# One expert stage of a two-block model kernel: 64 of 512 tokens by gathered rows, 448 by dense products with sums kept in PSUM

## The reference, cut to what matters

```python
s1 = einsum('thc,hkc->thk', q[:, :, 0], sub_keys1); s2 = einsum('thc,hkc->thk', q[:, :, 1], sub_keys2)
v1, i1 = top_k(s1, 16); v2, i2 = top_k(s2, 16)
vc, ic = top_k((v1[..., :, None] + v2[..., None, :]).reshape(T, 8, 256), 16)
idx = e1 * 128 + e2                     # per token: 8 heads x 16 picks
gate = softmax(vc)
pre = einsum('td,tkd->tk', x, expert_u[idx])
out = einsum('tk,tkd->td', gelu(pre) * gate, expert_v[idx])
```

## Time and profile before

| What | Value |
|---|---|
| Median of 3 runs | 3835.03 us (3834.25 to 3838.55) |
| Profiled execution, first to last instruction | 3830.8 us (its own whole time is not listed apart from this span) |
| TensorE busy | 3606.3 us, 94% of the span |
| VectorE busy | 2645.0 us, 69% |
| ScalarE, GpSimd busy | 1414.4 us and 1412.7 us, 37% each |
| Mean granted TensorE clock | 0.976 of full speed |

### The profile page before, as it was taken

The page is one execution under the profiler, slowest core; times in us unless marked ns, Lnnn a source line. Parts: engine busy times, 40 slices in busy tenths (PEclk is TensorE's granted clock), DMA queues, the critical chain, the costliest instruction groups (busy, mean ns, idle before and its releaser), DMA issues. The chain is left out here.

```text
span 3830.8 us, 55657 instructions
## 1 busy us (share of the span) xinstructions
PE 3606.3 (94%) x18886; PEld 2929.9 (76%) x18886; DVE 2645.0 (69%) x5198; ACT 1414.4 (37%) x2042; POOL 1412.7 (37%) x608
## 2 busy tenths in 40 slices
PE   8878999999999899999998989889998989989999
PEld 5746787788888788888887766678887877668877
DVE  7654899988888699999997756674455026755440
ACT  2443233345545323233323247632223133753331
POOL 3023344333333344444442326432222322444443
PEclk9989999999999999999999999999999999999999
DMA  5403444345545755555544480232111114032322
GB/s 212 142 12 132 156 147 140 126 136 186 194 151 194 253 194 195 189 192 195 193 164 158 137 165 12 70 107 66 60 60 49 60 61 134 7 121 88 95 79 89
DMA packets 248451, 490.54 MB, mean 128 GB/s; under 512 B 49124, under 2 KB 125924, under 8 KB 243341
## 3 DMA queue, kind: packets, MB, share of 16 engines
q1 hardware_dynamic: 227660, 447.95, 35.7%
q10 hardware_dynamic: 20672, 41.07, 2.9%
HBM read 411.59 MB, written 73.68 MB: 127 GB/s over the span
## 5 line engine op out<-in xcount | busy, mean ns | idle before, releaser
L433 POOL TENSOR_TENSOR ahead_low<-w_raw,ahead_high 128x1024 fp32r<-128x1024 f32 (+1 forms) x159 | 420.8, 2647 | 888.0 <-ACT ahead_high L369 888.0
L229 PE MATMUL psum<-h_high,ahead_high 128*128 128x512 f32 (+1 forms) x1504 | 540.3, 359 | 1.5 <-POOL ahead_low L433 1.5
L230 PE MATMUL psum<-h_low,ahead_high 128*128 128x512 f32 (+1 forms) x1504 | 538.1, 358 | 0.0
L231 PE MATMUL psum<-h_high,ahead_low 128*128 128x512 f32 (+1 forms) x1504 | 535.8, 356 | 0.0
L1945 POOL TENSOR_TENSOR pick_u_low<-pick_u_raw,pick_u_high 128x1024 fp32r<-128x1024 f32 x128 | 309.6, 2419 | 558.5 <-ACT pick_u_high L2022 558.5
L1809 POOL TENSOR_TENSOR v_low<-v_raw,v_high 128x1024 fp32r<-128x1024 f32 x128 | 334.1, 2633 | 369.5 <-ACT v_high L1806 369.5
L369 ACT ACTIVATE ahead_high<-w_raw 128x1024 fp32r<-128x1024 f32 (+1 forms) x159 | 178.0, 1119 | 740.8 <-PE psum L231 704.7
L229 PE MATMUL psum<-h_high,pick_u_high 128*128 128x512 f32 x1024 | 414.8, 405 | 1.4 <-POOL pick_u_low L1945 1.4
L229 PE MATMUL psum<-a_high,v_high 128*128 128x512 f32 x1024 | 399.1, 390 | 10.2 <-DVE a_low L2267 10.2
L230 PE MATMUL psum<-h_low,pick_u_high 128*128 128x512 f32 x1024 | 404.2, 395 | 0.0
L231 PE MATMUL psum<-h_high,pick_u_low 128*128 128x512 f32 x1024 | 401.4, 392 | 0.0
(11 more groups left out here) (395 smaller groups left out, 7236.3 us busy)
## 6 DMA issues: line engine op xcount, KB each, us to landing
pick_u_raw<-in_expert_uT SPq DMA_DIRECT2D x128, 512.0 KB, 3.5
v_raw<-in_expert_v SPq DMA_DIRECT2D x128, 512.0 KB, 4.8
mod_w<-in_w_mod SPq DMA_DIRECT2D x88, 512.0 KB, 3.7
w_raw<-in_ffn_up SPq DMA_DIRECT2D x84, 512.0 KB, 3.5
gelu_dram<-pick_gelu ACTq DMA_DIRECT2D x128, 256.0 KB, 2.0
gates_dram<-gate_plane SPq DMA_DIRECT2D x32, 1024.0 KB, 7.5
p<-gelu_dram SPq DMA_DIRECT2D x128, 256.0 KB, 5.0
g<-gates_dram SPq DMA_DIRECT2D x64, 512.0 KB, 4.3
```

Of the source, the lines that this page charges most:

```text
L229: nc.tensor.matmul(bank, w_high, x_high, start=first, stop=False)
L230: nc.tensor.matmul(bank, w_high, x_low, start=False, stop=False)
L231: return nc.tensor.matmul(bank, w_low, x_high, start=False, stop=last)
L433: nc.gpsimd.tensor_tensor(w_low[r % 2][:, :, :], raw[r % n_raw][:, :, :], w_high[r % 2][:, :, :].bitcast(F32), ALU.subtract).then_inc(k.w_ ...
```

## The change

The last 64 tokens no longer go through the dense products. Token columns 448 to 511 are laid out as 128 partitions (64 tokens, twice: partition 64 and up hold the second half of a token's picks), so each has 64 picks per partition. For each pick one indirect DMA, issued by GpSimd, gathers 128 rows of 1024 floats, first of `expert_u`, later of `expert_v`. VectorE takes the dot product with the token's own row (64 times), ScalarE applies gelu, VectorE multiplies with the gate, and in the second stage VectorE adds each gathered value row times its weight (64 times). A ring of four buffers holds the rows. A float32 matmul with two stacked identities folds both halves and transposes, once per 128 columns of the model width.

The dense products run over 448 columns. There are 7 gate planes of 64 tokens in place of 8, so the parts of `stage_pick` are 64 chunks for finding, 56 for gates, 8 at the end. The tile that holds the gathered tokens is found first. A tile's transposes move from its last chunk to the third chunk of the following tile, its picks are copied half-way through the scan of the next. VectorE's one-hot tiles read their row of numbers from PSUM, and the first of the pair is made for four tokens in one instruction. The copies of the queries for scoring (L2079 and a DMA) go, and the token rows are transposed by 32 float32 matmuls (`turn_h`).

In `stage_values` the sums of all 128 chunks stay in PSUM, and VectorE adds each bank once at the end. The subtraction of the value weights moves from GpSimd to VectorE for all but two chunks. All loops of both stages are written out.

```diff
-        self.gelu = k.nc.dram_tensor("gelu_dram", (N_KEYS, N_KEYS, SEQ), F32).ap()
-        self.gates = k.nc.dram_tensor("gates_dram", (SEQ // GATE_TOK, N_KEYS, N_KEYS, GATE_TOK), F32).ap()
+        self.h_high = k.place("peer_h_high", H_HIGH, KD, SEQ, dtype=FR)
+        self.h_low = k.place("peer_h_low", H_LOW, KD, SEQ, dtype=FR)
+        self.row_ring = [k.place(f"peer_row{r}", at, D) for r, at in enumerate((H_HIGH + KD * SEQ, H_HIGH + KD * SEQ + D, H_LOW + KD * SEQ, H_LOW + KD * SEQ + D))]
+
+        self.gelu = k.nc.dram_tensor("gelu_dram", (N_KEYS, N_KEYS, DENSE), F32).ap()
+        self.gates = k.nc.dram_tensor("gates_dram", (PLANES, N_KEYS, N_KEYS, GATE_TOK), F32).ap()
...
-EIGHT = range(8)
-FIND_CHUNKS, GATE_CHUNKS, LAST_CHUNKS = 14, 16, 8
+ROW_TOK = 64
+DENSE = SEQ - ROW_TOK
+PLANES = DENSE // GATE_TOK
+FIND_TILES = (3, 0, 1, 2)
+FIND_CHUNKS, PLANE_CHUNKS, LAST_CHUNKS = 16, 8, 8
+GATES_AT = len(FIND_TILES) * FIND_CHUNKS
+LAST_AT = GATES_AT + PLANES * PLANE_CHUNKS
...
+ROW_PICKS = PICKS * ROW_TOK // P
+ROW_RING = 4
+DOTS_AFTER = (0, 3, 3, 2)
+DOTS_FOUND = sum(DOTS_AFTER)
...
+    def gather(self, pool, j):
+        if j == 0:
+            pool.wait_ge(self.own_in, 32)
+        if j >= ROW_RING:
+            pool.wait_ge(self.used, j - ROW_RING + 1)
+        rows, n = (self.u, j) if j < ROW_PICKS else (self.v, j - ROW_PICKS)
+        self.nc.gpsimd.indirect_dma_start(self.ring[j % ROW_RING][:, :], None, rows,
+                                          bass.IndirectOffsetOnAxis(ap=self.own[:, 0, n:n + 1].bitcast(U32), axis=0)).then_inc(self.row_in[j % ROW_RING], 16)
+
+    def wait_row(self, dve, j):
+        dve.wait_ge(self.row_in[j % ROW_RING], 16 * (j // ROW_RING + 1))
+
+    def dot(self, dve, n, h, product):
+        self.wait_row(dve, n)
+        self.nc.vector.scalar_tensor_tensor(product, self.ring[n % ROW_RING][:, :], 1.0, h, ALU.mult, ALU.mult, accum_out=self.pre[:, n:n + 1]).then_inc(self.used, 1)
+        dve.wait_ge(self.used, n + 1)
+
+    def add(self, dve, n, acc):
+        j = ROW_PICKS + n
+        self.wait_row(dve, j)
+        row = self.ring[j % ROW_RING][:, :]
+        if n == 0:
+            ins = self.nc.vector.tensor_scalar(acc, row, self.a[:, 0:1], None, ALU.mult)
+        else:
+            dve.wait_ge(self.used, j)
+            ins = self.nc.vector.scalar_tensor_tensor(acc, row, self.a[:, n:n + 1], acc, ALU.mult, ALU.add)
+        ins.then_inc(self.used, 1)
...
+            for c in range(N_KEYS):
+                if c == FIND_CHUNKS + 4:
+                    rows.spread(sp)
+                if c == 2 * FIND_CHUNKS:
+                    sp.dma_start(cond, t["cond"].rearrange("p (c y) -> p c y", y=CTX)).then_inc(cond_in, 16)
+                n, r = divmod(c - LEAD - GATES_AT, PLANE_CHUNKS)
+                if n >= 1 and r < STORE_PARTS:
+                    store_part(n - 1, r)
+                load_u(c)
+                if c == LAST_AT + LEAD:
+                    load_mod(0)
+                    load_mod(1)
+                if c > LAST_AT + LEAD:
+                    load_mod(c - LAST_AT - LEAD + 1)
+            last_mod = N_KEYS - LAST_AT - LEAD + 1
...
+            gathered = 0
+            for c in range(N_KEYS):
+                split(c)
+
+                i, r = divmod(c, FIND_CHUNKS)
+                many = 0
+                if c < GATES_AT:
+                    if r == 5 and i == 1:
+                        many = ROW_RING
+                    if r == 5 and i > 1:
+                        many = DOTS_AFTER[i - 1]
+                elif c == GATES_AT + 2:
+                    many = DOTS_AFTER[-1]
+                elif GATES_AT + LEAD <= c < GATES_AT + LEAD + n_gate:
+                    many = 1
+                for _ in range(many):
+                    rows.gather(pool, gathered)
+                    gathered += 1
...
+            def chunk(c):
+                pe.wait_ge(u_split, c + 1)
+                if c >= 2:
+                    pe.wait_ge(gelu_done, c - 1)
+                for d in range(KD):
+                    mm = split_product(nc, k.psum[:, 5 + c % 2, 0:DENSE], u_high[c % 2][:, d, :], u_low[c % 2][:, d, :],
+                                       f.h_high[:, d, 0:DENSE], f.h_low[:, d, 0:DENSE], d == 0, d == KD - 1)
                 mm.then_inc(pre_done, 1)
...
+            def turn_h():
+                for d in range(KD):
+                    to = k.psum[:, 4 + 3 * (d // 4), d % 4 * P:(d % 4 + 1) * P]
+                    for half in HALVES:
+                        for part, h in enumerate((f.h_high, f.h_low)):
+                            mm = nc.tensor.matmul(to[half, :], h[:, d, DENSE:SEQ].bitcast(F32), k.const("ident"), start=(part == 0), stop=(part == 1))
+                mm.then_inc(rows_turned, 1)
+
             pe.wait_ge(keys_in, 16)
-            pe.sem_inc(pre_done, 2)
-            pe.wait_ge(staged, 16)
-            score()
-            with pe.Fori(0, TILES - 1) as it:
+            score(0)
+            for i in range(len(FIND_TILES)):
                 for r in range(FIND_CHUNKS):
-                    if r == SCORE_CHUNK:
-
-                        pe.wait_ge(best_found, it + 1)
-                        pe.wait_ge(staged, it * 16 + 32)
-                        score()
-                    chunk(it * FIND_CHUNKS, r)
-                turn(it)
-            for r in range(FIND_CHUNKS):
-                chunk((TILES - 1) * FIND_CHUNKS, r)
-            turn(TILES - 1)
-            with pe.Fori(0, TILES) as it:
-                for r in range(GATE_CHUNKS):
-                    chunk(it * GATE_CHUNKS + gates_at, r)
-                    for q in range(per_chunk):
-                        spread(it, r * per_chunk + q)
+                    if r == SCORE_CHUNK and i + 1 < len(FIND_TILES):
+
+                        score(i + 1)
+                    chunk(i * FIND_CHUNKS + r)
+                    if i and r == TURN_CHUNK:
+                        turn(i - 1)
+                    if i == 0 and r == TURN_CHUNK:
+                        turn_h()
+            for q in range(n_gate):
+                chunk(GATES_AT + q)
+                if q == TURN_CHUNK:
+                    turn(len(FIND_TILES) - 1)
+                for g in range(per_chunk):
+                    spread(q * per_chunk + g)
...
+                if i == 0:
+                    nc.vector.scalar_tensor_tensor(rows.all[:, 0, :].bitcast(U32), out[0][:, :], float(N_KEYS), out[1][:, :], ALU.mult, ALU.add).then_inc(rows.found, 1)
+                    dve.wait_ge(picked, 1)
+                    nc.vector.tensor_copy(rows.all[:, 1, :], out[2][:, :]).then_inc(rows.found, 1)
+                    dve.wait_ge(h_rows_ready, 2)
+                for _ in range(DOTS_AFTER[i]):
+                    rows.dot(dve, dots, h_rows[:, :], products[:, :])
+                    dots += 1
...
+            dve.wait_ge(h_rows_ready, 3)
+            for q in range(n_gate):
+                for g in range(q * per_chunk, (q + 1) * per_chunk):
                     b = g % 2
-                    dve.wait_ge(summed, it * per_tile + (g + 1))
+                    if g >= 2:
+                        dve.wait_ge(summed, g - 1)
+                    n = slice(g * group, (g + 1) * group)
+                    nc.vector.tensor_tensor(hot1[b][:, :, :], iota.unsqueeze(1).to_broadcast([P, group, N_KEYS]),
+                                            f.picks[:, 0, n].unsqueeze(2).to_broadcast([P, group, N_KEYS]), ALU.is_equal)
                     for j in range(group):
                         n = g * group + j
-                        nc.vector.tensor_scalar(hot1[b][:, j, :], iota, own[:, 0, n:n + 1], None, ALU.is_equal)
-                        ins = nc.vector.tensor_scalar(hot2[b][:, j, :], iota, own[:, 1, n:n + 1], own[:, 2, n:n + 1], ALU.is_equal, ALU.mult)
+                        ins = nc.vector.tensor_scalar(hot2[b][:, j, :], iota, f.picks[:, 1, n:n + 1], f.picks[:, 2, n:n + 1], ALU.is_equal, ALU.mult)
                     ins.then_inc(hot_ready, 1)
-                dve.wait_ge(hot_ready, it * per_tile + per_tile)
-
-            V.restart(dve)
+                rows.dot(dve, dots, h_rows[:, :], products[:, :])
+                dots += 1
+                if q == 2 * TURN_CHUNK:
+                    store_picks(len(FIND_TILES) - 1)
...
+            def step(c):
+                if c >= 2:
+                    act.wait_ge(b.v_in[c % 4], 16 * (c // 4 + 1) + b.chunks_before)
+                    if c >= 4:
+                        act.wait_ge(done.sem, done.at(c - 3))
+                    b.round_v(act, c)
+                act.wait_ge(gated, c + 1)
+                if c >= 4:
+                    act.wait_ge(done.sem, done.at(c - 3))
+                nc.scalar.activation(a_high[c % 4][:, :], a_full[c % 4][:, :], ACT.Copy).then_inc(a_high_ready.sem, 1)
+
+            for c in range(N_KEYS):
+                step(c)
...
+            for n in range(ROW_RING, ROW_PICKS):
+                rows.gather(pool, ROW_PICKS + n)
...
+            def chunk(c):
```

(44 more changed lines are left out.)

474 lines of the change are left out of this document (207 added, 267 removed).

## The result

The changed kernel takes 3704.01 us (median of 4 runs, 3702.11 to 3708.9) where the kernel before took 3836.79 beside it: ratio 0.966, 95% interval 0.9648 to 0.9672. Its profiled span is 3700.3 us against 3830.8, so 130.5 us less. The forecast was 156 less.

A forecast was written before the change was run, and what follows sets the result against it. TensorE was taken to set the time, VectorE close behind in two of four windows. Values -78.1, last chunks -0.3, finding and gates -76.4, start -1.2 sum to -156 us: 3835 to 3679 us, own range 3660 to 3705.

The forecast's parts named there:

- Columns pay: Finding and gates: narrower matmuls shorten both windows from 811.4 to 735 us, 76.4 less, with TensorE waiting 26 us for VectorE.
- Values, -78.1: Value stage: 128 chunks each 0.63 us shorter, 80.6 us less, minus folds and a less covered tail; 78.1 us less.
- the line between 344 and 512 columns: Dense products: interpolating matmul pace between these widths gives 200.4 ns at 448 columns for values, 203.3 for the first stage.
- The tail behind TensorE: End of the value stage: a tail of squares that gets less cover, 0.6 us more.
- The folds: End of the value stage: 8 float32 folds, two records each at about 120 ns, 1.9 us more.
- Last eight chunks, -0.3: Last chunks before the values: 5.4 us less, but TensorE then waits 5.1 us longer; 0.3 us less.
- modulation chain: Between last chunks and values: modulation loads and VectorE's columns, a chain of 50.7 us that does not shrink.
- Start and rest: Start: 1.2 us less, as the copy of queries goes; what lies around the span was left as it is.
- Slower gathers: Rival, GpSimd: gathers hold its queue, deciding from 6.6 us each; at 7.3 us each the kernel takes 3886 us; chance 0.06.
- VectorE bounds the gates: Rival, gates: one-hots or dot still held by GpSimd's subtraction, step 7.7 us, 58 us more, 3737 us; chance 0.15.
- Columns don't pay: Rival, dense products: matmuls of 448 columns keep the pace of 512, kernel 3815 us; chance 0.02.
- VectorE not late: Rival, finding: fewer collisions or hidden dots shrink the 26 + 2 us to 4, kernel 3655 us; chance 0.08.

## Why the prediction was right, and where it was off

The forecast of 3679 (own range 3660 to 3705) stood beside 3704: the case was right, the size 25 us off, at the edge of its range. It forecast a gain of 156 us, and 130.5 were measured between the profiled spans. By its own steps:

- **Columns pay.** Gates and finding: forecast 735 us for the two windows, measured 735.1 (452.9 to 1188.0). First spread 364 us after VectorE's first scan, measured 362.6; wait 26, measured 25.6; step 6.65, measured 6.70. The gathers cost GpSimd 0.96 us each (1.5 taken), hidden. The eight dots took 14.8 us (16 taken), six of them 1.3 and two 3.5, and the rest of VectorE's work within 1 us of its 348; how the single terms of that rest came out was not measured.
- **Values, -78.1.** The term that was mis-sized. TensorE is the bound and VectorE at 59% (some 65% forecast), but the pace is 202.7 ns in place of 200.4: 3072 x 2.3 = 7 us. (The prediction gave VectorE 5.9 us of work a chunk before, which adds up durations that overlap; the earlier trace rows have 686.51/128 = 5.36.) The step that failed is the line between 344 and 512 columns. At 448 it is one of two paces, and neither lies on that line. The tail behind TensorE was given 0.6 us and took 4.4 more (17.5 against 13.1): with one chunk per visit the banks finish 0.82 us apart, GpSimd's four additions of squares (1.43 us from one to the next) fall behind, and TensorE waits 2.2 us for them. Its eight sums then take 5.2 us in place of 3.6, the first of them at a granted clock of 0.5. With two chunks per visit the tail was 13.6. The folds took no more than their 1.9 us: 625.8 less 3072 x 0.2027 leaves 3.1 us, with 1.5 for the half clock of the first chunk in it.
- **Last eight chunks, -0.3.** This step failed. I forecast 42.6 us of chunks and a gap of 15, with the modulation chain setting the end. Measured 53.4 and 14.8. The gap's number was right by luck, for a wrong reason: it hangs on GpSimd, whose two value subtractions the change had moved behind the last chunk and whose block end comes 5.65 us late after gathers. The 10.8 us in the chunks are, in the main, the context sums and one load. The sums took 3.6 us before and now 5.4 behind a wait of 2.95, 4.8 more. The wait for a u part that the DMA engines bring late is 3.9, and the chunk at half clock behind it 1.6 more. Moving the sums took out their whole 8.1 us, also the 3.6 that were in the forecast. The chain's 50.7 us I took as fixed, and it was (50.2 here, from the first load at 1191.63); that what holds it, 18 MB in 54 us, would hold the u loads too once a chunk took 4.9 us in place of 5.5, I had not asked.
- **Start and rest.** The start was to gain 1.2 us and lost 1.1; the rest of the kernel took 3.0 us more. Neither need be the change's: between kernels with the same instructions there, the first score came at 443.1 to 449.0 and the rest took 1797.6 to 1803.0.
- Sum of the misses: 2.3 at the start, -0.5 in finding and gates, 10.5 around the last chunks, 10.3 in values and tail, 3.0 in the rest: 25.6 of 25.5.
- **Rivals.** Slower gathers: refuted, 0.96 us against a threshold of 6.6. VectorE bounds the gates: not from PSUM, and from SBUF just not. Columns don't pay: refuted, 4.86 us a chunk and not 5.44. VectorE not late: refuted by the 25.6 us.

By the Trainium skill, SBUF — State Buffer, section "Who interferes with whom", a VectorE operation with two SBUF inputs contends with a GpSimd operation that reads SBUF, and one with at most one SBUF input, outside the two-port modes, does not. The trace agrees for the wide one-hot: beside the subtraction it takes 2.86 us with its row of numbers in SBUF, and never over 0.69 with that row in PSUM.

What stays open: what chooses between 202.7 and 206.7 ns, and why 448 columns have neither 200.0 nor one pace. The choice isn't made by the rows (both paces stand in kernels with them), nor by the granted clock, and the slower pace also stands with six matmuls to a bank in place of three.

## What to carry to other kernels

Removing work from an engine that is 98% busy but hides beside TensorE gave nothing by itself here; count it as room for what is to be moved there. When a change makes the covering work shorter, go through everything it covered (loads, squares, the end of a block) and ask which of them now ends last; here that was 15 us of 25. And where an edit moves a few operations behind the last matmul of a block, add what the block's end itself takes on that engine. Filling a wait with work is not free either when the work collides with the engine that is waited for: of the 14.7 us that three moved chunks filled, 4.7 came back.

## What was not expected of the hardware

- GpSimd's end of block comes 5.0 to 5.7 us after its last operation where the block has issued indirect gathers (5.6 in the block of the picks, 5.0 to 5.1 in that of the values), in every such block of every kernel here, even with the last gather tens of microseconds back; without gathers it comes within 0.1 us of the last operation.
- The value products of 448 columns have two paces, 202.7 and 206.7 ns, each constant through a stage of 3072 matmuls. The slower one came in 5 of 11 profiled value stages, and in one of four stretches of an execution that changed the width in between. At 320, 384 and 512 columns the time over the columns is 13.3 ns in every value stage profiled.
